# A hybrid decoder layer on one Trainium2 core: a DMA of 96 eight-byte reads is issued ahead of everything else

## The reference, cut to what matters

```python
h = rms_norm(x, norm_w, 1e-6)                 # x: 256 x 2048, float32
proj = h @ w_in                               # 2048 x 7704
(q_a, kc_a, vc_a, ks_a, vs_a, kw_a, vw_a, g_a, z_a, q_b, k_b, v_b, z_b) = split(proj)
o_a = nsa_mixer(q_a, kc_a, vc_a, ks_a, vs_a, kw_a, vw_a, g_a, cmp_pos, cmp_k_w1, ...)
o_b = diff_mixer(q_b, k_b, v_b, lam_q1, lam_k1, lam_q2, lam_k2, subln_w, ...)
mixed = concat(o_a * silu(z_a), o_b * silu(z_b))
y = x + mixed @ w_out
return rms_norm(y, final_norm_w, 1e-6)
```

## Time and profile before

| | before |
|---|---|
| median of 3 runs | 490.55 us (490.53 to 491.11) |
| the profiled execution's own time | 491.02 us |
| its span, first to last instruction | 489.2 us |
| TensorE busy | 479.8 us, 98% |
| VectorE busy | 357.9 us, 73% |
| ScalarE busy | 221.6 us, 45% |
| GpSimd busy | 45.8 us, 9% |
| HBM read | 105.20 MB, 219 GB/s over the span |
| SP's queue of DMAs | 16256 packets, 104.34 MB |
| ScalarE's queue of DMAs | 1440 packets, 2.96 MB |

### The profile page before, as it was taken

One profiled execution on the slowest core, in us unless ns is written; L12 is line 12 of the kernel. 1 busy time (PEld: TensorE's weight loads), 2 busy tenths in 40 slices (PEclk: granted clock), 3 DMA queues, 4 the chain that ended last, 5 costly groups with the idle time before them and its releaser, 6 DMA issues.

```text
span 489.2 us, 6491 instructions
## 1 busy us (share of the span) xinstructions
PE 479.8 (98%) x2554; PEld 387.9 (79%) x2554; DVE 357.9 (73%) x501; ACT 221.6 (45%) x299; POOL 45.8 (9%) x49
## 2 busy tenths in 40 slices
PE   8999999999999999999999999999999999999994
PEld 6888867777777888888888888888888888888883
DVE  4765978377595896998898857488897998444533
ACT  5747433234333455545344454664435443444331
POOL 1003400020202002020020000102000000203050
PEclk9999999999999999999999999999999999999998
DMA  8999967877889433244262425445775454655004
GB/s 272 413 421 419 373 249 319 311 319 305 310 318 370 161 124 149 91 166 173 87 238 106 173 86 184 171 142 203 280 322 175 169 178 182 250 214 208 1 0 172
DMA packets 17725, 107.71 MB, mean 220 GB/s; under 512 B 2208, under 2 KB 2848, under 8 KB 5792
## 3 DMA queue, kind: packets, MB, share of 16 engines
q1 hardware_dynamic: 16256, 104.34, 56.2%
q10 hardware_dynamic: 1440, 2.96, 1.6%
HBM read 105.20 MB, written 2.10 MB: 219 GB/s over the span
## 4 chain that ended last, share of the span: by engine, by line
PE 96%; DMA 1%; issue 0%; SPq 0%; DVE 0%; POOLq 0%; ACT 0%; DVEq 0%; POOL 0%; ACTq 0%
PE acc L1103 27%; PE acc L1105 26%; PE acc L1104 26%; PE S L1264 3%; PE O L1158 3%; PE S L1281 1%; PE acc L1139 1%; PE acc L1146 1%; DMA raw<-head 1%; PE acc L1142 1%; PE O L1311 1%; PE O L1299 1%; PE O L1301 1%; PE O L1300 1%; PE O L1184 0%
## 5 line engine op out<-in xcount | busy, mean ns | idle before, releaser
L718 DVE TENSOR_TENSOR wlo<-raw,whi 128x2048 fp32r<-128x2048 f32 x72 | 165.3, 2300 | 83.2 <-ACT whi L448 82.6
L448 ACT ACTIVATE whi<-raw 128x2048 fp32r<-128x2048 f32 x72 | 137.9, 1917 | 160.7 <-PE acc L1105 149.9
L1103 PE MATMUL acc<-whi,hT_hi 128*128 128x512 f32 x440 | 174.3, 396 | 0.0
L1104 PE MATMUL acc<-wlo,hT_hi 128*128 128x512 f32 x440 | 171.5, 390 | 0.0
L1105 PE MATMUL acc<-whi,hT_lo 128*128 128x512 f32 x440 | 171.4, 390 | 0.0
L1103 PEld LDWEIGHTS acc<-whi,hT_hi 128*128 128x128 f32 x440 | 82.6, 188 | 23.5 <-issue 6.7
L1105 PEld LDWEIGHTS acc<-whi,hT_lo 128*128 128x128 f32 x440 | 82.6, 188 | 17.6
L1104 PEld LDWEIGHTS acc<-wlo,hT_hi 128*128 128x128 f32 x440 | 82.7, 188 | 16.6
L398 POOL TENSOR_TENSOR stage<-stage,stage 128x512 f32<-128x512 f32 (+1 forms) x16 | 23.4, 1477 | 180.2 <-DVE stage L769 180.2
L530 ACT ACTIVATE e<-S,small 128x128 f32<-128x128 f32 (+1 forms) x48 | 19.6, 420 | 26.3 <-DVE small L815 26.3
L778 DVE STREAM_TRANSPOSE zT<-stage 32x256 f32<-32x256 f32 x64 | 27.9, 436 | 2.0
(11 more groups left out here) (186 smaller groups left out, 486.5 us busy)
## 6 DMA issues: line engine op xcount, KB each, us to landing
raw<-stream SPq DMA_DIRECT2D x72, 1024.0 KB, 4.9
row_raw<-stream SPq DMA_DIRECT2D x16, 1024.0 KB, 6.3
raw<-head SPq DMA_DIRECT2D x6, 512.0 KB, 9.5
x_nat<-x_rows SPq DMA_DIRECT2D x2, 1024.0 KB, 14.4
x_nat<-x_rows SPq DMA_DIRECT2D x1, 2048.0 KB, 9.1
xTs<-head SPq DMA_DIRECT2D x3, 512.0 KB, 9.9
raw<-head SPq DMA_DIRECT2D x4, 256.0 KB, 4.2
fw<-final_w ACTq DMA_DIRECT2D x1, 1024.0 KB, 5.9
```

The lines of the kernel that those rows point to most:

```text
L448: act.activation(whi[:, n % SPLIT, :], raw[:, n % RAW, :], ACT.Copy).then_inc(hi_ready, 1)
L718: dve.tensor_tensor(wlo[:, n % SPLIT, :], raw[:, n % RAW, :], whi[:, n % SPLIT, :].bitcast(f32), ALU.subtract)\
L1103: pe.matmul(acc_bank(n), xh, wh, start=k == 0, stop=False)
L1104: pe.matmul(acc_bank(n), xh, wl, start=False, stop=False)
```

## The change

Ahead of the DMA of `nw`, ScalarE's queue issues one more DMA: from `head`, seen as rows of 16384 floats (64 KB), it reads the first two floats of each row into a small tile `touch`, with nothing else reading that tile. Its semaphore is waited for by SP's queue ahead of its last wait.

```diff
+TOUCH = 16384
...
+        touch = sb("touch", [P, 2])
...
+        touched = sem("touched")
...
             sp.dma_start(out[P:2 * P, 0:2 * NB], x_nat[:, 1, 0:2 * NB]).then_inc(stored, 16)
+            sp.wait_ge(touched, 16)
             sp.wait_ge(stored, 16 * (N_OUT + 2))
...
         def _(act):
+            n = sum(piece_width(w) for w in FIRST) * P // TOUCH
+            act.dma_start(touch[0:n, :], head[0:n * TOUCH].rearrange("(n w) -> n w", w=TOUCH)[:, 0:2]).then_inc(touched, 16)
             act.dma_start(nw[:, :], norm_w).then_inc(nw_in, 16)
             act.wait_ge(warm_ready, 1)
```

## The result

| | before | after |
|---|---|---|
| median of 22 runs each | 490.74 us (490.29 to 491.35) | 491.48 us (490.54 to 492.60) |
| ratio | | 1.0015 (95% interval 1.0009 to 1.0021) |
| profiled execution, span | 491.02, 489.2 us | 492.26, 490.5 us |

**The kernel became slower by 0.15%, where 0.2% faster was forecast.** The median hides something: the 22 executions after fall into two groups, 11 from 490.54 to 491.25 us and 11 from 491.71 to 492.60, with nothing between. Of the 22 before none is above 491.35. The profiled execution of after, 492.26 us, is one of the upper group.

A forecast was written before the change was run, and what follows sets the result against it. TensorE, busy 98% of the span, was taken to bound the kernel, late head pieces costing it 1.22 us. Terms -1.22 + 0.35 = -0.87 us took the median 490.55 to 489.7 us; range 489.0 to 491.7.

The forecast's parts named there:

- x1 and after: Pieces of head behind x0 and w0 land sooner once touched, removing all TensorE waits after its first product: -1.22 us.
- the touches change nothing: Rival, chance 0.28: long packets at the start don't belong to pages, or touches come too late; 490.6 us.
- nw one place later: Start of ScalarE's queue: nw's issue moves from 0.73 to 1.14 us, 0.41 us later, at no cost.
- covered by w0's lateness: ScalarE's head: nw's delay hides in its wait for w0, 0.83 us, of which 0.42 is left.
- w0 and x0: First pieces on SP's queue, read beside the touches: +0.35 us, bounds -0.52 to +1.1.
- The touches hold up the start: Rival, chance 0.18: nw lands late behind 96 first reads, so ScalarE and the first product start late; 492.1 us.
- decision point: In the held-up-start rival, the lateness of nw beyond its issue from which the start is delayed: 0.42 us.
- a last clause: End of the held-up-start signs: perhaps a granted clock below 1.00 at the start; given no size.
- The signs that I named: 2 to 8 us well over 270 GB/s; w2 before 7.3, w4 before 9.3; TensorE idle once; first product near 5.21.
- the last sign: Sign of being right: a later piece, such as chunk 4's start at 28.36 us, comes earlier by the whole gain.
- the sum's frame: A microsecond won or lost at the start of TensorE's work reaches the end, unless another engine comes due first.
- the packets of the touches: The 96 reads take about 1 us over 16 engines, 0.06 us, at the low end; high end 6.6 us each.

The follow-up runs named there:

- f2: The changed kernel with f1's added wait, but the 96 reads taken from the end of the weight stream, nothing of head touched; 492.69 us, ratio 1.0035.
- f1: The changed kernel with one wait added, so that the touches land before SP's queue issues any piece of head; 492.93 us, ratio 1.0046.
- e4: The kernel before with 46 instead of 40 warm-up matmuls, no DMA changed; ratio 0.9991.
- f3: The changed kernel with f1's added wait, but head touched only every 128 KB, 48 reads; 492.71 us, ratio 1.0040.

## Why the time rises: nw second in its queue

The changed kernel once more (h1), and beside it **only the order of the two DMAs** (e1), **only the place that is read** (e2), **32 reads** (f4), **16 reads of neighbouring bytes** (g1, repeated as h2), and **nw issued later with no read added** (h3):

```diff
-            act.dma_start(touch[0:n, :], head[0:n * TOUCH]...).then_inc(touched, 16)
             act.dma_start(nw[:, :], norm_w).then_inc(nw_in, 16)
+            act.dma_start(touch[0:n, :], head[0:n * TOUCH]...).then_inc(touched, 16)       # e1
...
+            n = 32                                                                         # f4
...
+            act.dma_start(touch[0:16, :], head[0:32].rearrange("(n w) -> n w", w=2)).then_inc(touched, 16)   # g1, h2
...
-            act.dma_start(nw[:, :], norm_w).then_inc(nw_in, 16)
             act.wait_ge(warm_ready, 1)
             act.activation(small[:, 60:61], warm[:, 0:1], ACT.Copy)
+            act.dma_start(nw[:, :], norm_w).then_inc(nw_in, 16)                            # h3, no touches
```

e2 takes `far` of f2 without the wait.

> The changed kernel with the two first DMAs of ScalarE's queue swapped: nw first, then the touches. Theory A (the touches shorten the later pieces, and the loss comes from nw standing behind them: hT_hi waits for nw until 4.18 us, the first product starts at 5.35 and the 12 matmuls after it run at half pace): nw is back at about 3.1 us, the first product at 5.2 or before, w4 still near 9.8 us, no slow matmuls; the time is 0.8 to 1.3 us under the kernel before, 489.4 to 489.9. Rival B (the 96 reads as such crowd the start, wherever they stand in the queue): no gain, 490.5 to 491.5, w0 and w1 late.

> The changed kernel, with its 96 reads of 8 bytes at the same 64 KB distance taken from the end of the weight stream and not from head. Nothing of head is touched, the cost of the DMA stays. Theory A: hT_hi late as in the changed kernel (near 4.2 us), but the pieces as late as before (w2 7.9, w4 10.4 us), so both losses and no gain: 491 to 493. Rival C (the pieces come sooner for another reason than having been touched, such as how the queues interleave): w4 near 9.8 us again and the time of the changed kernel, 491.5.

> The changed kernel with 32 touches in place of 96: x0 to w4, the first 2 MB. If the reads themselves delay nw (0.6 us of its 1.08 us, beside 0.44 us of issue), then with a third of them hT_hi is released near 3.7 us instead of 4.18, w4 still comes near 9.8 us, and the time is 490.6 to 491.2, under the changed kernel's. Rival F (nw is late because it is second in its queue, whatever the number of reads): hT_hi near 4.1 us and 491.4.

> The changed kernel with 16 reads of 8 neighbouring bytes each (128 bytes of head in all) in place of the 96 at 64 KB distance. Theory G (nw is late because it is second in its queue and its packets then run beside those of w0, not because of what is read ahead of it): hT_hi released at 3.9 to 4.1 us, as with 32 touches (4.02). Rival A, what is left of it (each read of another 64 KB stretch costs time): hT_hi near 3.5 us, the 0.41 us of the issue alone. Time 490.9 to 491.5 in the first case, 490.8 in the second.

> The changed kernel once more, beside the three below on one chip. So far 11 of its 22 executions lay at 491.7 us or above, and 4 of 11 with the 96 reads taken elsewhere. Theory H (nw's lateness opens an idle gap on TensorE, and the clock comes late in part of the executions): again a third to a half of them at 491.7 or above, median 491.0 to 491.9.

> The kernel with 16 neighbouring reads ahead of nw once more: its hT_hi was as late (4.26 us) as the changed kernel's (4.18), yet only 1 of 10 executions lay at 491.7 or above. If the lateness seen in the profile is all that counts, its times match the changed kernel's of the same call, a third to a half at 491.7 or above; if the number of reads adds to it in executions without the profiler, it stays at 490.9 with hardly one in ten up there.

> The kernel before with the DMA of nw issued behind the tiny activation on warm instead of ahead of it. No read is added; nw's issue moves from 0.73 to about 1.2 us or, if the issue waits for the table load, to 2.5. Theory H: hT_hi released near 4 us (or 4.5), a gap on TensorE and a part of the executions at 491.7 or above, median 491 to 492. Rival A (the added reads do the harm): the time of the kernel before.

| kernel | reads, and where nw stands | hT_hi released | ratio to before | at 491.7 us or above |
|---|---|---|---|---|
| after, first 22 | 96, nw second | 4.18 us | 1.0015 (1.0009 to 1.0021) | 11 of 22 |
| h1, the same again | 96, nw second | 4.36 | 1.0011 (1.0001 to 1.0021) | 7 of 11 |
| e2 | 96 elsewhere, nw second | 4.24 | 1.0008 (0.9999 to 1.0017) | 4 of 11 |
| f4 | 32, nw second | 4.02 | 1.0008 (0.9998 to 1.0018) | 3 of 11 |
| g1 | 16 neighbours, nw second | 4.26 | 0.9995 (0.9986 to 1.0004) | 1 of 10 |
| h2, the same again | 16 neighbours, nw second | 4.37 | 1.0009 (1.0000 to 1.0018) | 6 of 11 |
| e1 | 96, nw first | 3.10 | 0.9998 (0.9989 to 1.0007) | 0 of 11 |
| h3 | none, nw alone, later | 3.07 | 0.9997 (0.9988 to 1.0006) | 0 of 11 |

Beside these, the kernel before has 4 of 155 executions at 491.7 or above, none above 491.85. Whatever is read ahead of nw, 16 or 96 reads, here or elsewhere, hT_hi comes 0.9 to 1.3 us late, and 32 of 76 executions lie in the upper group. With nw first in its queue (e1, h3), none of 22 does. No effect of the number of reads is seen: g1 alone looked as if there were one, and its repetition took that back. e1 also missed its expectation: with nw back in time it was to win what the touches save, 489.4 to 489.9 us, and it came out level with the kernel before (490.93 against 490.90), a second sign that there is nothing to win. h3 missed its own in an instructive way: the DMA does not wait for the table load, it is issued at 1.02 us instead of 0.73, and nw lands no later at all. So 0.3 us of issue is nothing, and one place later in the queue, issued at 1.17, costs about 1.1.

What makes second place dear is seen from f1, where SP's pieces are held back. DMA issues, us to landing, of f1 and of the changed kernel:

```profile
touch<-head ACTq DMA_DIRECT2D x1, 0.8 KB, 1.7
nw<-norm_w_t ACTq DMA_DIRECT2D x1, 8.0 KB, 1.6
```

```profile
touch<-head ACTq DMA_DIRECT2D x1, 0.8 KB, 2.7
nw<-norm_w_t ACTq DMA_DIRECT2D x1, 8.0 KB, 3.0
```

With the pieces held back, nw lands 1.6 us after its issue, though it is second and has 96 reads ahead of it. Beside the pieces it takes 3.0. Its packets in the changed kernel (ScalarE's queue, 3 to 3.5 us) come a microsecond after those of the earlier trace rows, when SP's queue moves longer rows (0.17 MB in 111 packets in the same window):

```profile
q10 hardware_dynamic: 104, 0.01, 14.1%
```

In the kernel before they run beside x0's short rows. In e1 it is the touches that stand second, and they are the late ones: 2.9 us to landing, 2.4 for nw. So it takes both, the second place and the traffic of the other queue; why the second DMA's packets begin only near 3 us no run shows. The Trainium skill, in "DMA: Bandwidth & Descriptors" under "Queues, rings and completion order", says that each DMA engine takes turns between the queues that have work, packet by packet (a packet there is a group of several descriptors). Nothing here speaks against that, but no run shows the turns themselves, and they alone would not say why the second DMA starts late.

## Why the pace is slow: the gap, and the clock

Now the DMAs are left as they are, and only the number of warm-up matmuls changes, in the kernel before (g2, e4 and its repetition h4, g3) and in the changed kernel (i2, e3, i1, with 36, 46 and 50):

```diff
-WARM_UP, WARM_COLS = 40, 104
+WARM_UP, WARM_COLS = 46, 104      # or 36, 50, 52
```

> The changed kernel with 46 instead of 40 warm-up matmuls, so that TensorE has work until about 5.2 us, just before the first product at 5.35. Theory A: the slow pace of the 12 matmuls after 5.35 us comes from the idle gap of 0.66 us before them; with the gap closed they run at 0.23 us each in nearly every execution, the two groups of times (near 490.9 and near 492.1) become one, and the time is 489.5 to 490. Rival D (the pace does not hang on the gap; the slow matmuls are limited by the late pieces or by ScalarE): slow matmuls as before, 491.3 to 491.8.

> The kernel before with 46 warm-up matmuls, the control to the run above. Theory A: its gap of 0.53 us mattered little, its clock was already up at 5.2 us in most executions; the same within 0.3 us, 490.3 to 490.8, less spread. If the gap costs the kernel before too in some executions, it gains a few tenths, 490.2.

> The kernel before with 36 instead of 40 warm-up matmuls: nothing but TensorE's idle gap ahead of the first product grows, from 0.53 to 0.9 us. Theory H (the second group of times, near 492.1, comes from the gap, through the clock): a good part of the executions at 491.7 to 492.6 although no DMA is changed, median 491 to 492. Rival D (it comes from the transfers): all executions at 490.3 to 491.4 as with 40.

> The kernel before with 52 warm-up matmuls. With 46 the executions lay between 490.34 and 491.04 (before: 490.45 to 491.85 in the same hours). Theory H: with more of them the clock is up in still more executions, but at the low pace they end at 1.04 + 52 x 0.091 = 5.8 us and hold the first product up by 0.5 us where the clock is late: 490.4 to 490.7, no better than 46.

> The kernel before with 46 warm-up matmuls once more, the one version under both kernels so far (ratio 0.9991). If that holds, 0.3 to 0.4 us under the kernel before again and none of its executions above 491.2; if it was chance, the same time.

> The changed kernel with 50 warm-up matmuls, which at the low pace last until 1.04 + 50 x 0.091 = 5.6 us, past the first product of every look at a late nw so far (5.20 to 5.54). Theory H: the idle gap is gone in all executions, and at most one of eleven lies at 491.7 or above, where 32 of 76 did with 40 matmuls and a DMA ahead of nw; median 490.8 to 491.2. Rival D (the slow executions don't come from the gap): four or five of eleven up there again.

> The changed kernel with 36 warm-up matmuls, the gap near 1 us. Theory H: more executions at 491.7 or above than with 40, eight or more of eleven, median 492. Rival D: four or five of eleven.

| warm-up matmuls | DMAs of before: at 491.7 or above, ratio | a DMA ahead of nw: at 491.7 or above, ratio |
|---|---|---|
| 36 | 7 of 11, 1.0016 (1.0007 to 1.0025) | 5 of 6, 1.0032 (1.0020 to 1.0044) |
| 40 | 4 of 155 | 32 of 76, after: 1.0015 |
| 46 | 0 and 1 of 11, 0.9991 (0.9982 to 1.0000) and 0.9998 (0.9989 to 1.0007) | 1 of 11, 1.0000 (0.9991 to 1.0009) |
| 52 (before), 50 (a DMA ahead) | 0 of 11, 1.0000 (0.9991 to 1.0009) | 0 of 11, 1.0000 (0.9991 to 1.0008) |

Taking four warm-up matmuls from the kernel before, with no DMA changed, gives the very loss of the change (1.0016 against 1.0015). Adding six or ten to the changed kernel takes the loss away. Fewer warm-up matmuls mean less work before the first product as well as more idle time, so these runs alone would leave both as the cause; but the changed kernel and e1 have the same 40 and the same DMAs in another order, and there it is nw's lateness, and with it the idle time, that differs (18 of 33 executions in the upper group against 0 of 11). **So the upper group comes from the time that TensorE stands idle between the warm-up and the first product.** The timeline of the changed kernel with 46 (e3), TensorE:

```profile
1.03 4.17 PE L1347 MATMUL acc<-warm 128*128 128x104 bf16 x46 [1.03 <-DVE warm L718]
5.26 0.78 PE L1145 MATMUL acc<-whi,hT_hi 128*128 128x512 f32 x2
5.88 0.63 PE L1148 MATMUL acc<-whi,hT_lo 128*128 128x512 f32 x2
6.34 0.62 PE L1152 MATMUL acc<-wlo,hT_hi 128*128 128x512 f32 x2
```

And of e1, 40 warm-up matmuls and nw first, where no idle time was left either:

```profile
4.69 1.19 PE L1145 MATMUL acc<-whi,hT_hi 128*128 128x512 f32 x2
5.68 1.05 PE L1148 MATMUL acc<-whi,hT_lo 128*128 128x512 f32 x2
6.53 0.80 PE L1152 MATMUL acc<-wlo,hT_hi 128*128 128x512 f32 x2
7.17 0.71 PE L1145 MATMUL acc<-whi,hT_hi 128*128 128x512 f32 x2
```

The clock has two levels, 1.2 and 2.4 GHz. The warm-up runs for the most part at the low one: a matmul of 104 columns takes 3.65 / 40 = 0.091 us, near the 0.087 of 1.2 GHz. When the high level is reached can be read from the spacing of the pairs in every trace:

| traced execution | idle before the first product | first product | low level until | chunk 4 starts | its time |
|---|---|---|---|---|---|
| after | 0.66 us | 5.35 us | about 10 us | 29.42 us | 492.26 us |
| h1 | 0.85 | 5.54 | about 10 | 29.50 | 492.30 |
| e2 | 0.73 | 5.42 | 9.0 to 9.6 | 29.14 | 491.89 |
| f4 | 0.52 | 5.20 | before 5.2 | 27.68 | 490.43 |
| g1 | 0.91 | 5.43 | before 5.4 | 27.78 | 490.59 |
| h2 | 0.93 | 5.54 | before 5.5 | 27.98 | 490.94 |
| i2 (36) | 1.23 | 5.56 | before 5.6 | 27.77 | 491.17 |
| before | 0.53 | 5.21 | before 5.2 | 28.36 | 491.02 |
| g2 (36) | 0.36 | 4.64 | before 4.7 | 27.67 | 491.30 |
| e1 | none | 4.69 | 6.5 to 7.2 | 28.18 | 490.98 |
| h3 | none | 4.54 | 4.5 to 5.4 | 28.24 | 490.98 |
| i1 (50) | none | 5.33 | 6.3 to 7.0 | 28.36 | 491.22 |
| e3, e4, g3, h4 (46, 46, 52, 46) | under 0.1 | 4.59 to 5.50 | before 5.9 | 27.75 to 28.21 | 490.57 to 491.04 |

Three things are in it. Of the executions in the table, the three whose time lies in the upper group are the three in which the high level came only at 9 us or later. Without idle time the level can still be low at the first product, as in e1 and i1, but there it rose by 7 us; with idle time it was either up by the first product or stayed low for about 4 us more. And the late first product costs nothing by itself: f4, g1, h2 and i2 start it 0.5 to 1 us later than e1 or h3, and chunk 4 no later; the waits for late pieces in between are shorter by as much. It is a matter of chance which level comes: h2 had a gap of 0.93 us and the high level, and so had f1 to f3 with 1.6 to 2.2. That the chance grows with the length of the gap is not shown: the one trace of g2 had 0.36 us, and 7 of its 11 executions are in the upper group, against 32 of 76 with gaps of 0.5 to 0.9 in the traces. Nor is a warm-up that should fill the gap quite safe: e3 and h4 have one execution each at 492.0, whose cause no trace shows.

The Trainium skill, "TensorE: Matmul & The Clock Gate", Part 1, says that the transition point, at which the clock rises, varies from run to run for one and the same kernel. The groups of times here agree, and in the traces of these kernels the rise lies anywhere from before 4.7 to about 10 us.

No version beat the kernel before clearly. e3 and g3 had been expected to, at 489.5 to 490 and 490.4 to 490.7 us, and measured 490.82 and 491.08. With 46 warm-up matmuls the kernel before was at 0.9991 once and 0.9998 in the repetition, whose interval holds 1.

## Why the prediction was wrong, step by step

- **"x1 and after", -1.22 us: the step that failed.** It took the 1.1 us of first packets at 207 us for a cost of first reads that a touch would take over, though I wrote that no row could tell. f1 against f2 shows nothing taken over, and e1, with nw in time, won nothing. The measured gain of the touches is 0. The rival "the touches change nothing", at 0.28, was right about the touches, and the row that spoke for it, full rate on fresh memory from 9 to 12 us, was the one to follow.
- **"nw one place later", 0.41 us: mis-sized.** It was 1.08, since only the issue was counted and not what the second place costs beside the other queue's traffic (1.6 us to landing without the pieces, 3.0 with them).
- **"covered by w0's lateness, 0.83 us": one trace taken for the rule.** In five further traces of kernels whose nw comes as before (e4, g2, g3, h3, h4) w0's copy began at 3.99, 3.86, 3.84, 3.77 and 3.74 us, not at 4.44. ScalarE waits 0.2 to 0.5 us there for w0, and that is all the cover; TensorE's usual gap is near nothing, not 0.53. w4, too, began to be copied anywhere from 9.73 to 10.31 there; the 10.42 of the trace I read was the latest of all. So the 1.22 us that I meant to win, and the 58 ns per KB behind them, are partly the chance of one execution. Its time doesn't give that away: 491.02 us is ordinary, as the median of all 155 executions of the kernel before is 490.94, and the 490.55 of the first three was low.
- **"w0 and x0", +0.35 us:** in the profiled execution the product came 0.14 us later than the earlier trace rows, but against the usual start, near 4.7 us, 0.5 to 0.8 later. That is nw's doing and not w0's: w0 was there when ScalarE came to it, at 4.59 us. For a held-up w0 nothing was measured.
- **"The touches hold up the start":** the right place, with its decision point of 0.42 us past the issue (0.64 were measured), and the wrong price. I let the reads themselves be slow, and put the clock into a last clause. A gap of 0.7 us costs nothing visible by itself; through the clock it costs 1.2 us (the middle of the upper group, 492.1, less that of the lower, 491.0) in two executions of five. No term of the sum stood for that.
- **The signs that I named misled.** The changed kernel showed most of them: 1.75 MB from 2 to 8 us (292 GB/s), TensorE idle once, the first product within 0.4 us, w2 copied from 7.39 us. (w4, at 9.79, missed its 9.3.) But e4, g2 and h3 move 1.75 to 1.83 MB there with nothing touched. Only the last sign, the start of chunk 4, told the truth: later, not earlier.
- What held: the sum's frame (a shift at the start passes to the end: 1.06 us at chunk 4, 1.15 at the last matmul), that the packets of the touches are some 0.06 us per engine, and that the issue takes 0.41 us.

## What to carry to other kernels

When a kernel starts on a warm-up, look at the idle time between the last warm-up matmul and the first product: here that was what changed the time, and a tiny DMA put ahead of the one that everything waits for can open it. Read several traces before an idle time in the first microseconds is booked as cover or as gain: from one to the next it moved here by as much as the whole effect. Try a supposed cause by itself before it is built on: one run with the touches finished first and one with them elsewhere were enough here to tell that there is nothing to win.

## What the runs showed that was not expected

- **A second small DMA in a queue landed late although it carried 8 KB:** 2.7 to 3.2 us after its issue beside the pieces, 1.6 to 1.8 without them, with 16 or 96 reads ahead of it alike.
- **The column of the granted clock did not show the slow stretch.** Windows of the changed kernel, columns as in the earlier trace rows:

```profile
5.35:9.75 4.40, 4.40 (x10) 3.44 (x11) 3.75 (x7) 2.94 (x6) 0.00 (x0) 1.00 0.98 366
9.75:14.00 4.25, 4.25 (x19) 3.52 (x18) 2.85 (x3) 2.64 (x3) 0.00 (x0) 1.00 1.04 415
```

  Both say 1.00, but 10 matmuls start in the first 4.4 us and 19 in the next 4.25. At the very start the spacing of equal matmuls tells the clock, and that column doesn't.
- **The execution times of one and the same kernel fall into two groups 1.2 us apart**, and a change altered how often the upper one comes and hardly where they lie (the lower group after has its middle at 491.0 us, all executions before at 490.9).
